# Attention of an encoder trunk with the keys on the partitions, and a state scan in three operations a step

## The reference, cut to what matters

```
s = einsum('bgrqd,bgkd->bgrqk', qblk, kt) * scale        # scale = 128 ** -0.5
p = softmax(s, axis=-1)                                   # true maximum over all 1040 keys, float32
y_a = einsum('bgrqk,bgkd->bgrqd', p, vt) * silu(gate_a)
...
a_bar = exp(a * dt)                                       # complex, 64 groups x 64 states, two directions
_, states = lax.associative_scan(combine, (a_seq, bu))    # state[c] = a_bar * state[c-1] + bu[c]
```

## Time and profile before

| | us |
|---|---|
| median of 3 executions | 2870.61 |
| the profiled execution | 2863.34 |
| its span, first to last instruction | 2861.4 |
| stage `heads` | 548 to 906 |
| PE busy over the span | 2565.9 (90%) |
| DVE, ACT, POOL busy over the span | 1380.2, 963.4, 1102.8 |
| mean granted clock of PE | 0.956 of full speed |

### The profile page before, as it was taken

The page is one execution under the profiler, slowest core; times in us unless marked ns, Lnnn a source line. Parts: engine busy times, 40 slices in busy tenths (PEclk is TensorE's granted clock), DMA queues, the critical chain, the costliest instruction groups (busy, mean ns, idle before and its releaser), DMA issues. The chain is left out here.

```text
span 2861.4 us, 41418 instructions
## 1 busy us (share of the span) xinstructions
PE 2565.9 (90%) x15638; PEld 2213.8 (77%) x15638; DVE 1380.2 (48%) x2301; ACT 963.4 (34%) x1940; POOL 1102.8 (39%) x1228
## 2 busy tenths in 40 slices
PE   6999997799997765799979999999999699999698
PEld 6988886699996655677768888777777589999587
DVE  6464445677777732321654544545555422222314
ACT  4232223533334344133322222356565410000321
POOL 3444440277774003322035445334343345552320
PEclk9999999999998887999989999999999799999899
DMA  7323333101101444353433333443433454442543
GB/s 160 112 64 108 102 100 97 47 31 38 43 26 38 75 80 144 132 186 116 147 81 116 143 127 111 166 150 115 155 107 130 172 180 148 141 134 82 191 147 147
DMA packets 268361, 328.33 MB, mean 115 GB/s; under 512 B 45301, under 2 KB 216975, under 8 KB 267031
## 3 DMA queue, kind: packets, MB, share of 16 engines
q1 hardware_dynamic: 230006, 239.09, 27.8%
q10 hardware_dynamic: 38176, 86.78, 8.2%
HBM read 212.75 MB, written 103.55 MB: 111 GB/s over the span
## 5 line engine op out<-in xcount | busy, mean ns | idle before, releaser
L1013 POOL TENSOR_TENSOR w_hi<-w_raw,ones 128x512 fp32r<-128x512 f32 (+1 forms) x232 | 277.4, 1196 | 767.3 <-PE r L1024 263.2
L1015 POOL TENSOR_TENSOR w_lo<-w_raw,w_hi 128x512 fp32r<-128x512 f32 (+1 forms) x232 | 342.1, 1474 | 18.2
L1024 PE MATMUL r<-h_lo,w_hi 128*128 128x264 f32 (+1 forms) x864 | 286.6, 332 | 0.0
L1024 PE MATMUL r<-h_hi,w_lo 128*128 128x264 f32 (+1 forms) x864 | 278.5, 322 | 0.0
L1024 PE MATMUL r<-h_hi,w_hi 128*128 128x264 f32 (+1 forms) x864 | 277.6, 321 | 0.0
L1024 PE MATMUL r<-xc_lo,w_hi 128*128 128x264 f32 (+1 forms) x768 | 248.5, 324 | 28.4 <-POOL w_lo L1015 28.4
L1024 PE MATMUL r<-xc_hi,w_lo 128*128 128x264 f32 (+1 forms) x768 | 248.8, 324 | 0.0
L1024 PE MATMUL r<-xc_hi,w_hi 128*128 128x264 f32 (+1 forms) x768 | 248.2, 323 | 0.0
L434 POOL TENSOR_TENSOR w_lo<-w_raw,w_hi 128x512 fp32r<-128x512 f32 x64 | 85.7, 1364 | 250.4 <-ACT w_hi L500 250.1
L1024 PEld LDWEIGHTS r<-xc_lo,w_hi 128*128 128x128 f32 x768 | 145.9, 190 | 41.0 <-issue 29.0
L1024 PEld LDWEIGHTS r<-h_lo,w_hi 128*128 128x128 f32 x864 | 163.0, 189 | 16.4 <-issue 2.4
(11 more groups left out here) (347 smaller groups left out, 6377.1 us busy)
## 6 DMA issues: line engine op xcount, KB each, us to landing
w_raw<-in_w_in_even SPq DMA_DIRECT2D x72, 256.0 KB, 2.9
w_raw<-in_w_in_odd SPq DMA_DIRECT2D x64, 256.0 KB, 3.4
w_raw<-in_w_ogate SPq DMA_DIRECT2D x64, 256.0 KB, 7.1
v_d<-vs ACTq DMA_DIRECT2D x8, 1152.0 KB, 4.2
us<-u_d SPq DMA_DIRECT2D x128, 65.0 KB, 2.8
xc_d<-xc ACTq DMA_DIRECT2D x8, 1040.0 KB, 6.3
qk_d<-qk ACTq DMA_DIRECT2D x16, 520.0 KB, 2.7
sz_d<-sz SPq DMA_DIRECT2D x8, 1040.0 KB, 5.1
```

The source lines that it names most:

```text
L1013: self.nc.gpsimd.tensor_tensor(hi, raw, one, ALU.mult).then_inc(self.hi_done, 1)
L1015: self.nc.gpsimd.tensor_tensor(lo, raw, hi.bitcast(F32), ALU.subtract).then_inc(self.split, 1)
L1024: ins = self.nc.tensor.matmul(bank[:, 0:n], w[:, u % self.buffers, k, :], z[:, off:off + n], start=(first and k == 0 and w is self.hi and ...
```

## The change

Attention is turned: keys lie on the partitions from the start, so `prob` is never transposed.
- The keys are cut in nine tiles of 116 (the last 112; `KEYS`), the queries of a head in two parts of 580 and 460 columns (`PARTS`), of 5 and 4 tiles of 116 and 115 rows. A unit n is now one part of one head: 16 units, each with nine blocks j of keys. v has a column of ones beside its 128 (`HD + 1`), which makes the row sum in the same product.
- PE `scores(n, j)`: keys stationary, 580 or 460 queries moving. ACT `keep` copies the block to SBUF. DVE `higher` keeps a running maximum `top`, elementwise, over the nine blocks (8 operations a unit, both operands in SBUF).
- PE `turn_top`, DVE `find`: `top` is transposed (4 or 5 transposes), reduced to one maximum a query and set on a diagonal (`corner`). PE `spread` multiplies it by ones, so that it stands in all partitions. DVE `lower` subtracts it from the nine blocks (one operand in SBUF, one in PSUM), ACT `power` takes exp in place.
- PE `mix`: `prob` stationary, v and its ones moving (129 columns): output rows are queries. ACT `take_rows` copies them, DVE `invert` takes 1/sum, ACT `scale_rows` applies it, PE `turn_rows` transposes the rows, DVE `out` gates them.
- In a round n of the written order stand the scores of unit n, the maximum and the subtraction of unit n-1 and the mix of unit n-2; there are 19 rounds.
- The recurrence has one multiplication of 128 x 256 elements (Z once by each half of `step`) and two additions to the next Z, each waiting for the one before.
- q and gate are loaded, and the result stored, in parts, all by SP.

```
+KEYS = [(i * 116, min(116, L - i * 116)) for i in range(NT)]
+PARTS = [(0, 580, 5, 116), (580, 460, 4, 115)]
+START = (222, 0)
+HALVES = ([(0, 290), (290, 290)], [(0, 460)])
...
-            vt = se.sb("v", [P, NT, KV * HD])
+            vt = se.sb("v", [P, NT, KV, HD + 1])
...
-    with do.loop(CH // 2, 8) as i:
+    with do.loop(CH // 2, 6) as i:
         for b in range(2):
-            now = t["Z"][:, bass.ds(i * 2 + b, 1), :, :].rearrange("p k q g -> p (k q) g")
+            now = t["Z"][:, bass.ds(i * 2 + b, 1), :, :]
             nxt = t["Z"][:, bass.ds(i * 2 + (b + 1), 1), :, :].rearrange("p k q g -> p (k q) g")
             gp.sem_inc(turns, 1)
-            do.free(tt(tmp[:, 0], now, t["step_re"][:, :, :], ALU.mult))
-            do(tt(tmp[:, 1], now, t["step_im"][:, :, :], ALU.mult))
-            do(tt(tmp[:, 0], tmp[:, 0], tmp[:, 1, ::-1, :], ALU.add))
+            do(tt(tmp[:, :, :, :], now.broadcast_to([P, 2, 2, G]),
+                  t["step"][:, :, :].rearrange("p (o q) g -> p o q g", o=2), ALU.mult))
+            do(tt(nxt, nxt, tmp[:, :, 0, :], ALU.add))
             gp.sem_inc(turns, 1)
-            do(tt(nxt, nxt, tmp[:, 0], ALU.add))
+            do(tt(nxt, nxt, tmp[:, :, 1, :], ALU.add))
...
+    LOWERED = {0: ((2, 8),), 3: ((1, 0),), 4: ((1, 1), (1, 2)), 5: ((1, 3),), 6: ((1, 4), (1, 5)), 7: ((1, 6),),
+               8: ((1, 7),)}
...
+                def scores(n, j):
+                    off, width, tiles, m = PARTS[n % 2]
+                    ko, kn = KEYS[j]
+                    g = n // 2 % KV
+                    if j == 0:
+                        pe.wait_ge(q_done, n + 1)
+                        if n >= 2:
+                            pe.wait_ge(found, n - 1)
+                        if n and turned_in[n - 1]:
+                            pe.wait_ge(yd, turned_in[n - 1])
+                    elif j == 1:
+                        if n >= 2:
+                            pe.wait_ge(low, NT * (n - 1))
+                    else:
+                        pe.wait_ge(kept, NT * n + j - 1)
+                    out = region(n, j)
+                    for o, w in HALVES[n % 2]:
                         for x, z in ((0, 1), (0, 0), (1, 0)):
-                            last = nc.tensor.matmul(sreg[0:m, PO + o:PO + o + w], q[x][:, g, off:off + m],
-                                                    kr[z][:, g, o:o + w], start=(z == 1), stop=(x == 1))
-                        if o:
-                            last.then_inc(sc, 1)
...
+                            last = nc.tensor.matmul(out[0:kn, START[n % 2] + o:START[n % 2] + o + w],
+                                                    kr[z][:, g, ko:ko + kn], q[x][:, off + o:off + o + w],
+                                                    start=(z == 1), stop=(x == 1))
+                    last.then_inc(sc, 1)
...
+                def mix(n, j):
+                    off, width, tiles, m = PARTS[n % 2]
+                    g = n // 2 % KV
+                    for x in range(j * tiles, (j + 1) * tiles):
+                        i, k = divmod(x, NT)
+                        w = DONE[n] + i
+                        if i == 0:
+                            pe.wait_ge(ex, NT * n + k + 1)
+                        if k == 0 and w >= 2:
+                            pe.wait_ge(taken, w - 1)
+                        kn = KEYS[k][1]
+                        last = nc.tensor.matmul(o_slot(w)[0:m, :], sb[0:kn, n % NB, k, i * m:(i + 1) * m],
+                                                vt[0:kn, k, g, :], start=(k == 0), stop=(k == NT - 1))
+                        if k == NT - 1:
+                            last.then_inc(pv, 1)
...
+                pe.wait_ge(ones_set, 1)
+                for n in range(LAST + 1):
+                    for j in range(NT):
+                        if n < NU:
+                            scores(n, j)
+                        if j == 2 and 1 <= n <= NU:
+                            spread(n - 1)
+                        if 2 <= n < LAST:
+                            mix(n - 2, j)
+                        for w in turned_at.get(n * NT + j, ()):
+                            turn_rows(w, n)
+                        if j == 0 and 1 <= n <= NU:
+                            turn_top(n - 1)
...
+                def keep(n, j):
+                    kn, width = KEYS[j][1], PARTS[n % 2][1]
+                    if j == 0 and n >= NB:
+                        act.wait_ge(pv, DONE[n - NB + 1])
+                    act.wait_ge(sc, NT * n + j + 1)
+                    nc.scalar.activation(sb[0:kn, n % NB, j, 0:width],
+                                         region(n, j)[0:kn, START[n % 2]:START[n % 2] + width],
+                                         ACT.Copy).then_inc(kept, 1)
+                def power(n, j):
+                    kn, width = KEYS[j][1], PARTS[n % 2][1]
+                    act.wait_ge(low, NT * n + j + 1)
+                    nc.scalar.activation(sb[0:kn, n % NB, j, 0:width], sb[0:kn, n % NB, j, 0:width], ACT.Exp,
+                                         scale=SCALE).then_inc(ex, 1)
...
+                def higher(n, j):
+                    kn, width = KEYS[j][1], PARTS[n % 2][1]
+                    dve.wait_ge(kept, NT * n + j + 1)
+                    now = sb[0:kn, n % NB, j, 0:width]
+                    if j == 1:
+                        if n:
+                            dve.wait_ge(tt, n)
+                        v.tensor_tensor(top[0:kn, 0:width], sb[0:kn, n % NB, 0, 0:width], now,
+                                        ALU.max).then_inc(raised, 1)
+                    else:
+                        dve.wait_ge(raised, (NT - 1) * n + j - 1)
+                        v.tensor_tensor(top[0:kn, 0:width], top[0:kn, 0:width], now, ALU.max).then_inc(raised, 1)
+                def find(n):
+                    off, width, tiles, m = PARTS[n % 2]
+                    dve.wait_ge(tt, n + 1)
+                    out = region(n, NT)
+                    for at, i0, i1 in TOP_RUNS[n % 2]:
+                        ins = v.tensor_reduce(peak[0:m, i0:i1],
+                                              out[0:m, at:at + (i1 - i0) * KEYS[0][1]].rearrange(
+                                                  "p (i k) -> p i k", k=KEYS[0][1]), AX, ALU.max)
+                        do.free(ins)
+                    dve.wait_ge(steps, do.base + do.n)
+                    if n:
+                        dve.wait_ge(sp_done, n)
+                    v.tensor_tensor(corner[0:m, 0:width].rearrange("p (i k) -> p i k", k=m),
+                                    c["ident"][0:m, 0:m].unsqueeze(1).broadcast_to([m, tiles, m]),
+                                    peak[0:m, 0:tiles].unsqueeze(2).broadcast_to([m, tiles, m]),
+                                    ALU.mult).then_inc(found, 1)
+                def lower(n, j):
+                    kn, width = KEYS[j][1], PARTS[n % 2][1]
+                    if j == 0:
+                        dve.wait_ge(sp_done, n + 1)
+                    dve.wait_ge(kept, NT * n + j + 1)
+                    x = sb[0:kn, n % NB, j, 0:width]
+                    at = SPREAD_AT[n % 2]
+                    v.tensor_tensor(x, x, region(n, NT + 1)[0:kn, at:at + width], ALU.subtract).then_inc(low, 1)
+                def invert(w):
+                    m = PARTS[spot[w][0] % 2][3]
+                    dve.wait_ge(taken, w + 1)
+                    if w >= 4:
+                        dve.wait_ge(scaled, w - 3)
+                    v.reciprocal(inv[0:m, w % 4:w % 4 + 1], o_raw[0:m, w % 2, HD:HD + 1]).then_inc(got, 1)
+                def out(w, now):
+                    n, i = spot[w]
+                    off, width, tiles, m = PARTS[n % 2]
+                    if i == 0:
+                        dve.wait_ge(gl[n % 2], 16 * (n // 2 + 1))
+                    dve.wait_ge(tu, w + 1)
+                    y = gate[:, off + i * m:off + (i + 1) * m]
+                    v.tensor_tensor(y, y, region(now - 1, NT)[:, 0:m], ALU.mult).then_inc(yd, 1)
+                v.memset(vt[:, :, :, HD:HD + 1], 1.0).then_inc(ones_set, 1)
...
+                for n in range(LAST + 1):
+                    for j in range(NT):
+                        if j == 1 and 1 <= n <= NU:
+                            find(n - 1)
+                        for w in mixed_at.get(n * NT + j - 1, ()):
+                            invert(w)
+                        for w in out_at.get(n * NT + j, ()):
+                            out(w, n)
+                        for back, k in LOWERED.get(j, ()):
+                            if 0 <= n - back < NU:
+                                lower(n - back, k)
+                        if n < NU and j:
+                            higher(n, j)
+                        if j == 5 and n + 1 < NU:
+                            rest(n + 1)
```

More of the change, by code:

```diff
@@ L1569, in heads @@
     REP = HEADS // KV
[L1570 to L1580 removed]
+    NU, NB = 2 * HEADS, 3
@@ new lines, in heads @@
```

(30 more changed lines are left out.)

266 lines of the change are left out of this document (116 added, 150 removed).

## The result

| | before | changed |
|---|---|---|
| median, us | 2867.21 (2863.02 to 2874.99, 5 runs) | 2847.19 (2844.07 to 2850.46, 5 runs) |
| profiled execution; its span | 2863.34; 2861.4 | 2844.07; 2842.2 |
| first scan operation | 548.4 | 546.8 |
| scan | 349.8 | 346.4 |
| attention's last gate ends | 902.6 | 883.1 |

The ratio is 0.9926, 95% interval [0.9907, 0.9945]: 20 us faster, where 6.6 were forecast (2864 against 2870.61). Of the 19.2 us between the two spans 12.1 lie ahead of the next stage's begin (1.6 of them ahead of the first scan operation), 5.4 in that next stage, `s5_outputs`, and 1.7 behind it. `y_d` is the tensor in DRAM to which ACT's queue stores that stage's output.

The account below looks back on a forecast made before the run. Attention and POOL's scan end 4.4 us apart at one barrier; afterwards the scan (307 + 44 = 351 us) ends the stage, the next begins 5.4 us earlier, giving 2864 us; own range 2855 to 2873, 8 in 10 2847 to 2883.

Parts of the forecast that it names:

- Outside the stage nothing changes but tile widths of v: All stages other than the one with attention and scan: no change in time was counted there.
- The scan without disturbance: POOL's recurrence with no DVE beside it: 2.36 us a step, 307 us for 130 steps, against 321 before.
- The unseen gap: POOL's idle time where the first addition waits with register work and no increment: 0.19 us, between 0.08 and 0.27.
- The disturbance: Delay of POOL's scan by DVE operations with both operands in SBUF: 44 us (38 to 50), against 28.7 before.
- The scan's sum: POOL's scan in all: 307 + 44 = 351 us, as before (350), ending at 899.4.
- the barrier: Between the stage's last arrival and the next stage: 1 us, 0 at least, 3.2 with a store at most.
- Attention off the path: Attention takes 34.7 us a head on PE, ends at about 856 to 880 and waits for the scan.
- rival 2: Attention ends last, PE waiting in each round at turn_top and spread; with 4 us a round 2897; chance 0.1.
- The margin: Time attention ends ahead of the scan and waits for it at the stage's end: some 20 to 40 us.
- 1 (the scan disturbed no more): POOL's scan is disturbed no more than before, 28.7 us; next stage at 885, total 2849 to 2850; chance 0.2.
- 3: Each DVE operation with two SBUF inputs costs the scan its whole length, 112 us; total 2933; chance 0.05.
- 4: The undisturbed scan is not shorter, a step of 2.44 us; next stage at 910.4, total 2875; chance 0.12.

Follow-up runs that it names:

- a2: The changed kernel run once more, unchanged, for a second profile: 2844.77 us, ratio 0.9932 to the kernel before.
- e2: The changed kernel with the old scan of four operations put back: 2862.27 us, ratio 0.9990 to the kernel before.
- e3: The changed kernel with only 20 of the 130 scan steps, its recurrence left incomplete: 2830.91 us, ratio 0.9874 to the kernel before.
- e5: The changed kernel with the running maximum reading its new block from PSUM instead of the SBUF copy: 2835.23 us, ratio 0.9884 to the kernel before.
- e7: The changed kernel with 44 PE products (ones by identity) behind its attention: 2856.05 us, ratio 0.9955 to the kernel before.
- e9: The changed kernel with attention's stores of output rows issued by ScalarE instead of SyncE: 2847.15 us, ratio 0.9938 to the kernel before.
- e10: The kernel before with 22 small PE products (88 instructions) spread over its attention: 2856.81 us, ratio 0.9973 to the kernel before.
- e1: The kernel before with the new scan of three operations, attention as before: 2863.93 us, ratio 0.9998 to the kernel before.
- e4: The kernel before with v stored 129 columns apart instead of 128, nothing else: 2865.72 us, ratio 1.0002 to the kernel before.
- e6: The kernel before with 32 more POOL operations behind the scan: 2871.84 us, ratio 1.0018 to the kernel before.
- e8: The kernel before with attention's eight output stores issued by SyncE instead of ScalarE: 2864.81 us, ratio 1.0002 to the kernel before.
- e13: The changed kernel with 64 small PE products (8 columns, 256 instructions) behind its attention: 2860.31 us, ratio 0.9986 to the kernel before.
- e11: The changed kernel with 36 PE products (ones by identity, 128 columns) behind its attention: 2847.71 us, ratio 0.9940 to the kernel before.

## Why the prediction was wrong, point by point

The forecast was 2864 us with a range of its own of 2855 to 2873; 2847.19 were measured, at the edge of the wider range of 2847 to 2883. On the terms of the profiles it is a span of 2856.0 against 2842.2: 6.5 us lie in the stage, about 5.5 in S5 outputs and 1.7 behind it.

- **"Outside the stage nothing changes but tile widths of v"** is the largest step that failed: a term put at nothing, which measured 5.4 to 7.5 us in S5 outputs. The change takes some 900 instructions out of PE's stream (926 ahead of the first product of `yp`), so all the stages behind stand elsewhere in its 16 KB blocks. Five profiles with the old attention have 165.0 to 167.8 us there, the seven with the new one in the changed kernel, a2, e2, e3, e5, e7 and e9 159.9 to 162.0; the old one moved by 88 instructions has 158.9. That the place has an effect is shown by e10; how far it goes is shown for the last round (1.7 us) and not for the slower clock in the rounds before. I had looked at nothing outside the stage.
- **The scan without disturbance**: a step 2.35 us, forecast 2.36. The unseen gap is 0.19 (row at 892.10), as taken. Right; the 256-wide multiplication is 0.72, right.
- **The disturbance**: 41.1 and 42.6 us, forecast 44 (38 to 50). Right in kind and in size: all of it lies on POOL operations that overlap `higher`, `corner` or q_lo; the 68 that overlap `lower` and none of these take 0.002 us over the undisturbed length on average. Timelines of the changed kernel, POOL and then DVE:

```profile
643.54 0.77 POOL L801 TENSOR_TENSOR Z<-Z,scan 128x128 f32 x1 [0.18 <-POOL Z L799]
...
648.11 0.46 POOL L799 TENSOR_TENSOR Z<-Z,scan 128x128 f32 x1 [0.19 <-POOL scan L797]
...
651.27 0.74 POOL L801 TENSOR_TENSOR Z<-Z,scan 128x128 f32 x1 [0.18 <-POOL Z L799]
...
643.92 0.89 DVE L1815 TENSOR_TENSOR top<-prob 116x460 f32<-116x460 f32 x1
...
647.69 0.76 DVE L1845 TENSOR_TENSOR prob<-prob,long 116x580 f32<-116x580 f32 x1
...
651.07 0.63 DVE L1819 TENSOR_TENSOR top<-top,prob 116x460 f32<-116x460 f32 x1
```

  Under L1819 POOL's operation ends 0.31 us behind DVE's; under L1845 (one operand in PSUM) the one at 648.11 keeps its 0.46. DVE's L1815 takes 0.89 and not 0.63: it began while POOL's at 643.54 ran. The Trainium skill ("SBUF — State Buffer", Who interferes with whom) lets such a pair exclude each other for a whole instruction. The price on POOL was 0.26 us an operation (41.1/160), less than an operation's length: in these rows DVE's 0.63 us cost POOL 0.28 (0.74 for 0.46), since POOL's began 0.20 behind DVE's, and of its own 0.46 only 0.31 followed DVE's end. In e5 the operand's place took it away (41 to 9.6 us).
- **The scan's sum**: 351 forecast, 346.4 and 347.8 measured, a term 3 to 5 us too large; it began at 546.8 and 547.3, not 548.4 (548.4, 547.4 and 547.2 in three kernels with the old attention: scatter). The next stage so began 6.5 us before the 900.4 forecast: 1.6 by the start, 4.6 by the scan, 0.3 by the barrier (0.7, not 1).
- **Attention off the path**: the stage did end with the scan, and rival 2 did not come. But attention ended at 883.1, past 856 to 880. A head takes 39.6 us, not 34.7, and 38.3 in e3 and e5, where POOL hardly disturbs DVE. PE was busy for 297.1 us in the stage and not about 280. About 3.9 us of a head are idle PE (28.7 of 294 us); the waits of PE in the changed kernel from 600 to 860 us:

```profile
PE long L1729 <- DVE gate L1861: 5.4, 7, 0.8
PE short L1691 <- DVE top L1819: 5.1, 7, 0.8
PE long L1729 <- issue: 5.0, 7, 0.9
```

  These are the turns of rows, two in a row at a round's start, each waiting for the gate of the one before, and turn_top, which I had expected not to wait. The margin was 10 us (14 in the second profile) and not the 20 to 40 forecast.
- **The rivals**: 1 (the scan disturbed no more) was wrong in its reason, 41 us and not 28.7, though the time fell near the 2849 to 2850 that it gave: close to the right number for the wrong reason, since it had the next stage at 885 and not at 893.9 or 895.7. 3 and 4 did not come, by the rows above: disturbance 41 and not 112, and an undisturbed step of 2.35 us and not 2.44.
- What stays open: in "all behind", 1786.2 to 1787.5 us where a stage stands in its blocks about as in the changed kernel (8 profiles), 1787.8 to 1795.3 elsewhere (8 profiles). Which starts there meet a fetch was not traced, and scatter is as large: before, e1, e4, e6 and e8 have one stream of PE and lie between 1788.0 and 1795.3. That a fetch makes the starts long is argued from 27 coincidences in 27 and from e10, where the starts were rid of both; why it should hold up other engines' starts was not found.

## What to carry to other kernels

When two chains end within a few us of each other, one shortened alone gives nothing: the next stage began 0.1 us earlier with the new scan alone, 5.7 later with the new attention alone (which lengthens the scan), and 10 to 12 earlier with both. Work out both ends before dropping either. If POOL runs a chain of operations that wait for one another, have DVE read one operand from PSUM beside it where it lies there anyway. And before a difference of 0.3% is put down to an edit, add a few dozen PE instructions that compute nothing in front of the later stages: 88 of them made this program 8 us faster (e10).

## What the runs showed of the hardware

- A `y_d` start takes 0.31 to 0.54 us on ACT's queue; of 43 that begin within 0.42 us of a 16 KB fetch of PE's instructions 27 take 1.08 to 1.91 us, and SP's starts at those moments 0.88 to 2.04.
- A POOL operation under a DVE operation with two SBUF operands ends 0.31 us behind it, one under `lower` (one operand in PSUM) is not longer (rows above), and DVE is delayed in turn (0.89 us for 0.63).
- A PE that is busy throughout can lose its clock where its products are narrow. The added products of e13 (8 columns), in two windows, and those of e7 (128 columns):

```profile
884.20:888.00 3.80, 3.80 (x36) 3.80 (x35) 0.27 (x1) 0.00 (x0) 2.55 (x5) 0.98 0.17 62
888.00:908.10 20.10, 20.10 (x95) 20.05 (x94) 0.00 (x0) 0.00 (x0) 4.89 (x9) 0.50 0.00 1
```

```profile
881.30:891.20 9.90, 9.90 (x89) 9.76 (x88) 0.28 (x1) 0.00 (x0) 6.86 (x14) 1.00 0.07 25
```

  PE is busy throughout in all three. The narrow products began at full clock (2.4 GHz), where they take 3.8/36 = 0.11 us an instruction, as the wide ones do (9.9/88); then the clock fell to 0.50 (1.2 GHz) and stayed there while they went on, at 20.1/95 = 0.21 us each. The wide ones kept 1.00 to their end. This is one profile of each; e11's 36 wide products also kept 1.00.
